# Two fused norm and projection stages: most of their opening loads are issued later, behind the first tile's expert rows

## The chip, the cores and the metric

One core of one Trainium2 chip runs the whole program as one launch. The time is that of the device in microseconds, median of several runs. The engines are TensorE (PE in the profile), VectorE (DVE), ScalarE (ACT), GpSimd (POOL) and SyncE (SP). SP and ACT issue ordinary DMAs, POOL issues the indirect ones (gathers). All of them move their bytes through the same 16 DMA engines.

## The reference, cut to what matters

Two transformer blocks of depth two and one, over 1024 tokens of width 1024 in float32. Each layer is a mixer (attention and the like), a norm, a mixture of experts and a norm. The change touches two places, each between the experts of one layer and the mixer of the next:

```python
y = hierarchical_moe(h, ...)                        # out[token] = g0 * rows[p0] + g1 * rows[p1]
x = layer_norm(ALPHA * x + (1 + g2) * y, ln_g, ln_b)
# next layer
h = x * (1 + sc1) + sh1
qkv = h @ w_qkv                                     # or h @ w_in in the third layer
```

Every token has two rows among the experts' outputs, at places that the router found at run time. `g2`, `sc1` and `sh1` are vectors of 1024 numbers that `front` computed and left in DRAM, `ln_g` and `ln_b` are inputs.

## The kernel before, in words

The program is a row of stages, each with its own buffers and semaphores and with a barrier of all engines at its end. The two stages of this change are `norm_qkv` (stage `n1`, lines 811 to 1081) and `norm_mix` (stage `n3`, lines 1084 to 1429). Each starts after an experts stage and works through 8 tiles of 128 tokens. For each tile `t`:

1. POOL gathers the tile's two expert rows per token, `z` and `y2` (L884, L1171), 0.52 MB each. From `t = 2` on it first waits until the norm's output of tile `t - 2` has been stored, since that lies in `y2` (semaphore `x_st`).
2. ACT scales `z` by the first gate (`weigh`, L937, L1261). DVE adds `y2` times the second (L1010, L1364), multiplies by `gate` (L1015, L1369), adds alpha times `x` (L1017, L1371), takes the statistics and normalises (`combine`).
3. DVE makes two results: `xt`, the shaped input of the projection (L1028, L1382), and `y2`, the norm's output (L1030, L1384). PE turns `xt` by transposes (`turn_h`), ACT copies it (`spread_h`), and PE projects it with the weights `wt` (`project`). ACT keeps the result, and DVE works on it: `rope` in `norm_qkv`, ending at L1071, `norm_latents` in `norm_mix`, ending at L1410. PE turns what they leave (`turn_qk`, `turn_lat`).

For tile 0, DVE also adds 1 to `gate` (L1013, L1367) and folds the five constants together (`shape_next`, L1035 to L1038, L1389 to L1392), before `xt` and `y2` can be made.

The order of the loads is written out by hand. SP issues in this order: `places`, `gates`, `x` of tiles 0 and 1, the constants `gate`, `g`, `b`, `bs`, `gs` (0.52 MB each, since one row is spread over 128 partitions), `ident`, the weights in 3 or 4 column groups (6.3 and 6.8 MB), the rotation tables and gains (in `norm_mix` behind the first group of weights), in `norm_mix` also `uq` and `ukv`. Then comes a loop over the tiles, which stores the norm's output (`x_out`, L869, L1151) and loads `x` of tile `t + 2`. An instruction of this queue that doesn't find room, or waits, holds all behind it.

ACT works in a fixed order, too: in each turn of its loop `weigh(t + 2)` comes first, and the copies of tile `t`'s products come behind it. So do DVE and PE: in `norm_qkv` DVE does `combine(t + 2)` and then `rope(t)`, in `norm_mix` it does `norm_latents(t)` and then `combine(t + 2)`. PE does in `norm_qkv` `project(t, 0)`, `project(t, 1)`, `turn_qk(t - 1)`, `turn_h(t + 1)`, `project(t, 2)`, and in `norm_mix` `project(t, 0)`, `turn_q(t - 1)`, `project(t, 1)`, `turn_lat(t)`, and so on.

Of the kernel before, what the change touches and what calls it, by code (L numbers as in the profile page):

```python
# [16 lines left out]
P = 128  # L17
# [793 lines left out]
def norm_qkv(nc, name, x, mod, part, ln_g, ln_b, alpha, x_out, experts, nxt, w, q_gain, k_gain, a, qT, kT, v, scale):  # L811
# [6 lines left out]
    row = lambda m, n: m[0, n * D:(n + 1) * D].partition_broadcast(P)  # L818
    out_rows = x_out.rearrange("(r g c) n -> g r c n", g=TILES, c=GRID_W // TILES)
    with Stage(nc, name) as st:  # L820
# [12 lines left out]
        id_in, e_in, c_in, t_in, tables, shaping = (st.sem(n) for n in ("id_in", "e_in", "c_in", "t_in", "tables", "shaping"))  # L833
        w_in = [st.sem(f"w_in{c}") for c in range(GROUPS)]
        x_in, y_in, x_st = ([st.sem(f"{n}{j}") for j in range(2)] for n in ("x_in", "y_in", "x_st"))
        ready, weighted, nv, rt, sd, h_ready, x_ready = (st.sem(n) for n in ("ready", "weighted", "nv", "rt", "sd", "h_ready", "x_ready"))
        turned, evac, mm_done, qkv_cp, squared = (st.sem(n) for n in ("turned", "evac", "mm_done", "qkv_cp", "squared"))
        rv, roots, rope_done = (st.sem(n) for n in ("rv", "roots", "rope_done"))
# [11 lines left out]
        with st.block() as block:  # L850

            @block.sync
            def _(sp):
                sp.dma_start(places[:, :, :], experts[1]).then_inc(e_in, 16)
                sp.dma_start(gates[:, :, :], experts[2]).then_inc(e_in, 16)
                for j in range(2):
                    sp.dma_start(xt[:, j], x[j * P:(j + 1) * P, :]).then_inc(x_in[j], 16)
                for dst, src in ((gate, row(mod, part)), (g, ln_g.partition_broadcast(P)), (b, ln_b.partition_broadcast(P)),
                                 (bs, row(nxt[0], nxt[1])), (gs, row(nxt[0], nxt[1] + 1))):
                    sp.dma_start(dst[:, :], src).then_inc(c_in, 16)  # L860
                sp.dma_start(ident[:, :], a["ident"]).then_inc(id_in, 16)
                for c in range(GROUPS):
                    sp.dma_start(wt[:, :, c * 512:(c + 1) * 512], w.rearrange("(c p) n -> p c n", p=P)[:, :, c * 512:(c + 1) * 512]).then_inc(w_in[c], 16)
                for dst, src in ((cos[:, 0], rows(a["cos_grid"])), (sin[:, 0], rows(a["sin_grid"])),
                                 (gain[:, 0], q_gain.partition_broadcast(P)), (gain[:, 1], k_gain.partition_broadcast(P))):
                    sp.dma_start(dst, src).then_inc(t_in, 16)
                for t in range(TILES):
                    sp.wait_ge(x_ready, t + 1)
                    sp.dma_start(out_rows[t], y2[:, t % 2]).then_inc(x_st[t % 2], 16)  # L869
                    if t + 2 < TILES:  # L870
                        sp.wait_ge(turned, fills["h", t, 1] + 1)
                        sp.dma_start(xt[:, t % 2], x[(t + 2) * P:(t + 3) * P, :]).then_inc(x_in[t % 2], 16)
                for j in range(2):
                    sp.wait_ge(x_st[j], 16 * TILES // 2)

            @block.gpsimd
            def _(pool):
                pool.wait_ge(e_in, 32)
                for t in range(TILES):
                    if t >= 2:  # L880
                        pool.wait_ge(x_ready, t - 1)
                        pool.wait_ge(x_st[t % 2], 16 * (t // 2))
                    for k, dst in enumerate((z, y2)):
                        pool.indirect_dma_start(out=dst[:, t % 2], out_offset=None, in_=experts[0],  # L884
                                                in_offset=bass.IndirectOffsetOnAxis(ap=places[:, k, t:t + 1], axis=0)).then_inc(y_in[t % 2], 16)

            @block.tensor
            def _(pe):
# [115 lines left out]
            def _(dve):  # L1004
                step, shaped, turning = steps(dve, nv, 0), steps(dve, sd, 0), steps(dve, rv, 0)

                def combine(t):
                    j = t % 2
                    dve.wait_ge(weighted, t + 1)
                    step(dve.scalar_tensor_tensor(z[:, j], y2[:, j], gates[:, 1, t:t + 1], z[:, j], ALU.mult, ALU.add))  # L1010
                    if t == 0:
                        dve.wait_ge(c_in, 16 * 5)
                        dve.tensor_scalar(gate[:, :], gate[:, :], 1.0, None, ALU.add).then_inc(ready, 1)  # L1013
                        dve.wait_ge(ready, 1)
                    step(dve.tensor_tensor(z[:, j], z[:, j], gate[:, :], ALU.mult))  # L1015
                    dve.wait_ge(x_in[j], 16 * (t // 2 + 1))
                    step(dve.scalar_tensor_tensor(z[:, j], xt[:, j], alpha, z[:, j], ALU.mult, ALU.add))  # L1017
                    step(dve.bn_stats(bn[:, j, 0], z[:, j, 0:HALF]))
                    step(dve.bn_stats(bn[:, j, 1], z[:, j, HALF:]))
                    step(dve.bn_aggr(mv[:, j], bn[:, j]))  # L1020
                    step(dve.tensor_scalar(inv[:, j:j + 1], mv[:, j, 1:2], LN_EPS, None, ALU.add))
                    step(dve.reciprocal(inv[:, j:j + 1], inv[:, j:j + 1]))
                    if t == 0:
                        shape_next()
                    dve.wait_ge(rt, t + 1)
                    shaped(dve.tensor_scalar(z[:, j], z[:, j], mv[:, j, 0:1], rstd[:, j:j + 1], ALU.subtract, ALU.mult))
                    shaped(dve.tensor_tensor(xt[:, j], z[:, j], gs[:, :], ALU.mult))
                    dve.tensor_tensor(xt[:, j], xt[:, j], bs[:, :], ALU.add).then_inc(h_ready, 1)  # L1028
                    shaped(dve.tensor_tensor(y2[:, j], z[:, j], g[:, :], ALU.mult))
                    dve.tensor_tensor(y2[:, j], y2[:, j], b[:, :], ALU.add).then_inc(x_ready, 1)  # L1030

                def shape_next():

                    shape = steps(dve, shaping, 0)
                    shape(dve.tensor_scalar(gs[:, :], gs[:, :], 1.0, None, ALU.add))  # L1035
                    shape(dve.tensor_tensor(out[:, 0:D], b[:, :], gs[:, :], ALU.mult))
                    shape(dve.tensor_tensor(bs[:, :], bs[:, :], out[:, 0:D], ALU.add))
                    shape(dve.tensor_tensor(gs[:, :], gs[:, :], g[:, :], ALU.mult))  # L1038
# [45 lines left out]
def norm_mix(nc, name, x, mod, part, ln_g, ln_b, alpha, x_out, experts, nxt, w, q_gain, kv_gain, w_uq, w_ukv, a, padded, qT, kT, v, scale):  # L1084
# [9 lines left out]
    with Stage(nc, name) as st:  # L1094
# [16 lines left out]
        id_in, e_in, c_in, t_in, u_in, shaping = (st.sem(n) for n in ("id_in", "e_in", "c_in", "t_in", "u_in", "shaping"))  # L1111
        w_in = [st.sem(f"w_in{c}") for c in range(GROUPS)]
        x_in, y_in, x_st, v_st = ([st.sem(f"{n}{j}") for j in range(2)] for n in ("x_in", "y_in", "x_st", "v_st"))
        ready, weighted, nv, rt, sd, h_ready, x_ready = (st.sem(n) for n in ("ready", "weighted", "nv", "rt", "sd", "h_ready", "x_ready"))
        turned, evac, mm_done, pr_cp, lat_cp, summed = (st.sem(n) for n in ("turned", "evac", "mm_done", "pr_cp", "lat_cp", "summed"))
        lv, lat_root, lat_ready, up_done, up_cp, qv, q_ready = (st.sem(n) for n in ("lv", "lat_root", "lat_ready", "up_done", "up_cp", "qv", "q_ready"))
# [9 lines left out]
        with st.block() as block:  # L1126

            @block.sync
            def _(sp):
                sp.dma_start(places[:, :, :], experts[1]).then_inc(e_in, 16)  # L1130
                sp.dma_start(gates[:, :, :], experts[2]).then_inc(e_in, 16)
                for j in range(2):
                    sp.dma_start(xt[:, j], x[j * P:(j + 1) * P, :]).then_inc(x_in[j], 16)
                for dst, src in ((gate, row(mod, part)), (g, ln_g.partition_broadcast(P)), (b, ln_b.partition_broadcast(P)),
                                 (bs, row(nxt[0], nxt[1])), (gs, row(nxt[0], nxt[1] + 1))):
                    sp.dma_start(dst[:, :], src).then_inc(c_in, 16)
                sp.dma_start(ident[:, :], a["ident"]).then_inc(id_in, 16)
                for c in range(GROUPS):
# [22 lines left out]
            @block.gpsimd  # L1161
            def _(pool):
                pool.memset(zero[:, :], 0.0).then_inc(zeroed, 1)
                pool.memset(latn[:, :], 0.0).then_inc(blank, 1)
                pool.wait_ge(e_in, 32)
                for t in range(TILES):
                    if t >= 2:
                        pool.wait_ge(x_ready, t - 1)
                        pool.wait_ge(x_st[t % 2], 16 * (t // 2))
                    for k, dst in enumerate((z, y2)):  # L1170
                        pool.indirect_dma_start(out=dst[:, t % 2], out_offset=None, in_=experts[0],  # L1171
                                                in_offset=bass.IndirectOffsetOnAxis(ap=places[:, k, t:t + 1], axis=0)).then_inc(y_in[t % 2], 16)

            @block.tensor
            def _(pe):
# [182 lines left out]
            def _(dve):  # L1358
                step, shaped, latent, turning = steps(dve, nv, 0), steps(dve, sd, 0), steps(dve, lv, 0), steps(dve, qv, 0)

                def combine(t):
                    j = t % 2
                    dve.wait_ge(weighted, t + 1)
                    step(dve.scalar_tensor_tensor(z[:, j], y2[:, j], gates[:, 1, t:t + 1], z[:, j], ALU.mult, ALU.add))  # L1364
                    if t == 0:
                        dve.wait_ge(c_in, 16 * 5)
                        dve.tensor_scalar(gate[:, :], gate[:, :], 1.0, None, ALU.add).then_inc(ready, 1)  # L1367
                        dve.wait_ge(ready, 1)
                    step(dve.tensor_tensor(z[:, j], z[:, j], gate[:, :], ALU.mult))  # L1369
# [16 lines left out]
                def shape_next():  # L1386

                    shape = steps(dve, shaping, 0)
                    shape(dve.tensor_scalar(gs[:, :], gs[:, :], 1.0, None, ALU.add))  # L1389
                    shape(dve.tensor_tensor(y2[:, 0], b[:, :], gs[:, :], ALU.mult))  # L1390
                    shape(dve.tensor_tensor(bs[:, :], bs[:, :], y2[:, 0], ALU.add))
# [1694 lines left out]
```

## Time and profile before

| | us |
|---|---|
| median of 3 runs | 4115.12 (4114.41 to 4116.6) |
| the profiled execution | 4115.45 |
| its span | 4113.5 |
| PE busy (matmul) | 3484.4, 85% of the span |
| DVE busy | 1571.3, 38% |
| ACT busy | 873.8, 21% |
| DMA, mean over the span | 205 GB/s |
| stage `n1`, first instruction | 1347.12 |
| stage `n3`, first instruction | 2779.69 |

The profiled execution is 0.33 us above the median of the runs, inside their spread. PE is the busiest engine over the whole, but in the first 32 us of both stages it has nothing to do, and what counts there is when loads land.

### The profile page before, as it was taken

The numbers are of one execution on the slowest core, as the hardware profiler recorded it, in microseconds if no ns is written. First come the engines' busy times: TensorE is split into PE (matmuls) and PEld (weight loads), VectorE is DVE, ScalarE is ACT, GpSimd is POOL, SyncE is SP. The second block draws the span as 40 slices with busy tenths as digits, with TensorE's granted clock in tenths as the row PEclk, the third lists the DMA queues.
The fourth block names the chain that finished last, engine by engine and source line by source line (L and its number), as shares of the span: only waits on it lengthen the run. The fifth ranks groups of instructions, "written<-read, shape, count | busy, mean of one in ns | idle before, by whom it ended". The sixth has DMA issues, their size and how long they took to land. (4 is left out here: it accounts for less than half of the span.)

```text
span 4113.5 us, 48036 instructions
## 1 busy us (share of the span) xinstructions
PE 3484.4 (85%) x18756; PEld 1936.0 (47%) x18756; DVE 1571.3 (38%) x2595; ACT 873.8 (21%) x1896; POOL 235.5 (6%) x250
## 2 busy tenths in 40 slices
PE   7998988499999598999874999985999657847994
PEld 3444644144444244777442444433556456425662
DVE  4641755200000674666452000004426673551114
ACT  0001721011111123555110101002335322001112
POOL 1002000200000100000002000001000000011001
PEclk9999998699999799999986999997999878968997
DMA  9963031599996610000316999956210310419994
GB/s 379 357 220 122 7 130 66 209 427 426 426 422 256 201 57 1 1 1 2 140 56 239 427 426 427 421 227 213 88 46 23 112 46 22 159 36 366 420 390 195
DMA packets 176908, 842.26 MB, mean 205 GB/s; under 512 B 53455, under 2 KB 60367, under 8 KB 130610
## 3 DMA queue, kind: packets, MB, share of 16 engines
q1 hardware_dynamic: 142434, 737.83, 44.8%
q0 software_dynamic: 20576, 54.16, 3.6%
q10 hardware_dynamic: 13680, 47.24, 2.9%
q8 instruction: 152, 2.49, 0.2%
q14 instruction: 66, 0.54, 0.0%
HBM read 758.39 MB, written 97.20 MB: 208 GB/s over the span
## 5 line engine op out<-in xcount | busy, mean ns | idle before, releaser
L395 PE MATMUL front_acc<-front_hT,front_wt 128*128 128x512 f32 x512 | 224.8, 601 | 5.5 <-DMA front_wt<-in_na_w_qkv 5.5
L1215 PE MATMUL n_acc<-n_wt,n_hT 128*128 128x512 f32 (+2 forms) x512 | 191.3, 531 | 0.7 <-ACT n_hT L1255 0.7
L201 DVE TENSOR_REDUCE gqa_top<-gqa_scores 128x1 f32<-128x1024 f32 x128 | 150.8, 1220 | 101.5 <-PE gqa_scores L149 101.5
L232 ACT ACTIVATE gqa_probs<-gqa_scores,gqa_top 128x1024 f32<-128x1024 f32 x128 | 142.5, 1113 | 168.2 <-DVE gqa_top L201 168.2
L2137 PE MATMUL m1x_gp<-m1x_w,m1x_xT 128*128 128x512 f32 (+1 forms) x512 | 171.9, 600 | 1.5 <-issue 0.7
L2137 PE MATMUL m0x_gp<-m0x_w,m0x_xT 128*128 128x512 f32 (+1 forms) x512 | 171.4, 599 | 1.5 <-issue 0.7
L2162 PE MATMUL m1x_yp<-m1x_w,m1x_hidT 128*128 128x512 f32 (+1 forms) x512 | 169.3, 594 | 2.1 <-ACT m1x_hidT L2223 2.1
L2162 PE MATMUL m0x_yp<-m0x_w,m0x_hidT 128*128 128x512 f32 (+1 forms) x512 | 169.3, 594 | 2.1 <-ACT m0x_hidT L2223 2.1
L2137 PE MATMUL m0x_up<-m0x_w,m0x_xT 128*128 128x512 f32 (+1 forms) x512 | 168.8, 593 | 0.0
L2137 PE MATMUL m1x_up<-m1x_w,m1x_xT 128*128 128x512 f32 (+1 forms) x512 | 168.8, 593 | 0.0
L913 PE MATMUL n_acc<-n_wt,n_hT 128*128 128x512 f32 x384 | 168.2, 598 | 0.7 <-ACT n_hT L931 0.7
L395 PEld LDWEIGHTS front_acc<-front_hT,front_wt 128*128 128x128 f32 x512 | 97.9, 193 | 131.8 <-issue 131.1
L468 DVE SCALAR_TENSOR_TENSOR front_total<-v,front_cact,front_total 128x2048 f32<-128x2048 f32 x56 | 131.6, 2350 | 64.3 <-DMA v<-in_ada_w 44.8
L139 PE MATMUL gqa_turn<-gqa_ident,gqa_probs 128*128 128x128 f32 x1024 | 139.9, 280 | 0.8 <-DVE gqa_probsT L190 0.7
L2277 DVE TENSOR_TENSOR m1x_hid<-m1x_sg,m1x_up 128x512 f32<-128x512 f32 x24 | 16.5, 687 | 320.7 <-PE m1x_up L2137 320.7
L2277 DVE TENSOR_TENSOR m0x_hid<-m0x_sg,m0x_up 128x512 f32<-128x512 f32 x24 | 16.5, 688 | 320.2 <-PE m0x_up L2137 320.2
L139 PEld LDWEIGHTS gqa_turn<-gqa_ident,gqa_probs 128*128 128x128 f32 x1024 | 109.4, 140 | 60.0 <-issue 59.1
L1215 PEld LDWEIGHTS n_acc<-n_wt,n_hT 128*128 128x128 f32 x512 | 98.2, 194 | 82.9 <-issue 77.8
L149 PE MATMUL gqa_scores<-k1T,q1T 64*128 64x512 f32 x512 | 131.0, 627 | 5.9 <-DMA gqa_ident<-in_ident 3.4
L168 PE MATMUL gqa_out<-gqa_probsT,v 128*64 128x128 f32 x2048 | 125.9, 276 | 0.8 <-ACT gqa_probsT L228 0.8
L1707 PE MATMUL n_acc<-n_wt,o1T 128*128 128x512 f32 x256 | 112.9, 601 | 14.8 <-DMA n_wt<-in_gqa_w_o 14.8
L1707 PE MATMUL n_acc<-n_wt,mixT 128*128 128x512 f32 x256 | 112.7, 600 | 15.0 <-DMA n_wt<-in_w_out 15.0
(617 smaller groups left out, 5469.6 us busy)
## 6 DMA issues: line engine op xcount, KB each, us to landing
m0x_w<-in_moe_w_gate SPq DMA_DIRECT2D x32, 2048.0 KB, 33.3
m0x_w<-in_moe_w_up SPq DMA_DIRECT2D x32, 2048.0 KB, 33.2
m0x_w<-in_moe_w_down SPq DMA_DIRECT2D x32, 2048.0 KB, 33.4
m1x_w<-in_moe_w_gate SPq DMA_DIRECT2D x32, 2048.0 KB, 32.7
m1x_w<-in_moe_w_up SPq DMA_DIRECT2D x32, 2048.0 KB, 32.7
m1x_w<-in_moe_w_down SPq DMA_DIRECT2D x32, 2048.0 KB, 33.2
v<-in_ada_w SPq DMA_DIRECT2D x40, 1024.0 KB, 12.4
m2x_w<-in_moe_w_gate SPq DMA_DIRECT2D x32, 1024.0 KB, 32.2
```

Of the source, the lines that this page charges most:

```text
L139: last = pe.transpose(turn[f % TURN][:, i * P:(i + 1) * P], src, ident[:, :])
L149: last = pe.matmul(scores[h][:, c * 512:(c + 1) * 512], qT[half, j, t * P:(t + 1) * P], kT[half, 2 * j // SHARE, c * 512:(c + 1) * 512], s ...
L168: pe.matmul(out[h * HEAD:(h + 1) * HEAD, 0:P], v[:, k, kv * HEAD:(kv + 1) * HEAD], probsT[:, n % 2, h, k], start=k == 0, stop=k == TILES - 1)
L201: dve.tensor_reduce(top[:, n % 2, h:h + 1], scores[h][:, :], AX.X, ALU.max, negate=True).then_inc(max_ready, 1)
L232: act.activation(probs[:, n % 2, h], scores[h][:, :], ACT.Exp, bias=top[:, n % 2, h:h + 1], accum_out=total[:, n % 2, h:h + 1]).then_inc(p ...
L395: last = pe.matmul(acc[n % 4][:, :], wt[:, c % 2, k, i * P:(i + 1) * P], hT[:, k, half * 512:(half + 1) * 512], start=k == 0, stop=k == KC ...
L468: dve.scalar_tensor_tensor(total[:, q % 2], mw[:, s % RING], by, total[:, q % 2], ALU.mult, ALU.add).then_inc(weighed, 1)
L913: last = pe.matmul(acc[t % 2][:, c], hT[:, t % 2, k], wt[:, k, c * 512:(c + 1) * 512], start=k == 0, stop=k == KC - 1)
L1215: last = pe.matmul(acc[c][:, 0:n1 - n0], hT[:, t % 2, k], wt[:, k, n0:n1], start=k == 0, stop=k == KC - 1)
L1707: last = pe.matmul(acc[t % 2][:, c * HALF:(c + 1) * HALF], srcT[:, place(k), t * P:(t + 1) * P], wt[:, k, c * HALF:(c + 1) * HALF], start= ...
L2137: last = pe.matmul(acc[r, 0:F], xT[:, j, k, r], w[:, q % RING, k * F:(k + 1) * F], start=k == 0, stop=k == KC - 1)
L2162: last = pe.matmul(yp[e][r, :], hidT[:, k, r], w[:, q % RING, k * D + e * 512:k * D + (e + 1) * 512], start=k == 0, stop=k == FC - 1)
```

## The change

Both stages get two semaphores, `asked` and `gate_in`. POOL raises `asked` once it has issued the two gathers of tile 0. SP issues `places`, `gates` and `x` of tile 0, waits for `asked`, issues `gate` alone (counted by `gate_in`), waits until both gathers of tile 0 have landed (`y_in[0]` at 32), and only then issues `x` of tile 1, the other four constants (now `gs` first), `ident`, the weights and all the rest in the old order. DVE waits for `gate` alone where it waited for all five constants, and for the other four at the head of `shape_next`. Nothing is computed otherwise.

The part of `norm_qkv`; that of `norm_mix` is the same with its own lines (L1133 to L1138, L1171, L1366, L1388):

```diff
+        asked, gate_in = st.sem("asked"), st.sem("gate_in")
...
                 sp.dma_start(places[:, :, :], experts[1]).then_inc(e_in, 16)
                 sp.dma_start(gates[:, :, :], experts[2]).then_inc(e_in, 16)
-                for j in range(2):
-                    sp.dma_start(xt[:, j], x[j * P:(j + 1) * P, :]).then_inc(x_in[j], 16)
-                for dst, src in ((gate, row(mod, part)), (g, ln_g.partition_broadcast(P)), (b, ln_b.partition_broadcast(P)),
-                                 (bs, row(nxt[0], nxt[1])), (gs, row(nxt[0], nxt[1] + 1))):
+                sp.dma_start(xt[:, 0], x[0:P, :]).then_inc(x_in[0], 16)
+                sp.wait_ge(asked, 1)
+                sp.dma_start(gate[:, :], row(mod, part)).then_inc(gate_in, 16)
+                sp.wait_ge(y_in[0], 32)
+                sp.dma_start(xt[:, 1], x[P:2 * P, :]).then_inc(x_in[1], 16)
+                for dst, src in ((gs, row(nxt[0], nxt[1] + 1)), (g, ln_g.partition_broadcast(P)), (b, ln_b.partition_broadcast(P)),
+                                 (bs, row(nxt[0], nxt[1]))):
                     sp.dma_start(dst[:, :], src).then_inc(c_in, 16)
                 sp.dma_start(ident[:, :], a["ident"]).then_inc(id_in, 16)
                 for c in range(GROUPS):
...
                     for k, dst in enumerate((z, y2)):
                         pool.indirect_dma_start(...).then_inc(y_in[t % 2], 16)
+                    if t == 0:
+                        pool.sem_inc(asked, 1)
...
                     if t == 0:
-                        dve.wait_ge(c_in, 16 * 5)
+                        dve.wait_ge(gate_in, 16)
                         dve.tensor_scalar(gate[:, :], gate[:, :], 1.0, None, ALU.add).then_inc(ready, 1)
...
                 def shape_next():
                     shape = steps(dve, shaping, 0)
+                    dve.wait_ge(c_in, 16 * 4)
```

## Rows read from the trace of the kernel before

**Rows 1.** Waits of PE in both stages: who for whom, total us, times, longest
```profile
PE n_turn L894 <- DVE n_xt L1028: 46.0, 1, 46.0
...
PE n_turn L1181 <- DVE n_xt L1382: 45.5, 1, 45.5
```
**Rows 2.** Timeline, opening of `n1`: start, us, engine, line, [idle before <-releaser]
```profile
1347.98 0.90 SPq L857 DMA_DIRECT2D n_xt<-sc_x  x2
...
1349.36 0.96 POOL L884 DMA_INDIRECT n_z<-sc_expert_rows,n_places  x1 [98.26 <-DMA n_gates<-sc_gates]
...
1350.64 0.96 POOL L884 DMA_INDIRECT n_y<-sc_expert_rows,n_places  x1 [0.31 <-issue]
...
1351.90 15.62 SPq L863 DMA_DIRECT2D n_wt<-in_gqa_w_qkv  x3
...
1360.83 1.15 ACT L937 ACTIVATE n_z<-n_z,n_gates 128x1024 f32<-128x1024 f32 x1 [27.16 <-DMA n_y<-sc_expert_rows,n_places]
...
1365.63 0.69 DVE L1013 TENSOR_SCALAR n_gate<-n_gate 128x1024 f32<-128x1024 f32 x1 [2.34 <-DMA n_gs<-sc_mod]
...
1370.97 0.69 DVE L1035 TENSOR_SCALAR n_gs<-n_gs 128x1024 f32<-128x1024 f32 x1
...
1378.95 1.94 PE L894 MATMUL n_turn<-n_ident,n_xt 128*128 128x128 f32 x8 [45.98 <-DVE n_xt L1028]
```
**Rows 3.** Windows: us, busy of five engines, PEclk, DMA share, GB/s
```profile
1349.00:1351.00 2.00, 0.00 (x0) 0.00 (x0) 0.00 (x0) 0.00 (x0) 1.33 (x2) 0.50 0.83 285
...
1353.00:1355.00 2.00, 0.00 (x0) 0.00 (x0) 0.00 (x0) 0.00 (x0) 0.95 (x1) 0.50 1.03 330
...
1361.00:1363.00 2.00, 0.00 (x0) 0.00 (x0) 0.99 (x1) 0.98 (x1) 0.00 (x0) 0.50 1.02 418
...
1367.00:1381.00 14.00, 1.94 (x8) 1.56 (x8) 13.52 (x16) 2.09 (x4) 0.00 (x0) 0.50 1.05 386
...
1390.00:1392.00 2.00, 2.00 (x6) 0.90 (x5) 1.97 (x3) 0.00 (x0) 0.24 (x1) 1.00 0.76 254
...
2804.00:2807.00 3.00, 0.00 (x0) 0.00 (x0) 2.90 (x4) 0.00 (x0) 0.00 (x0) 0.50 0.31 62
...
2835.00:2838.00 3.00, 0.00 (x0) 0.00 (x0) 0.98 (x8) 2.36 (x8) 0.00 (x0) 0.50 0.42 168
```
**Rows 4.** Timeline of `n1` behind its opening, same columns
```profile
1382.58 0.63 SPq L869 DMA_DIRECT2D sc_x<-n_y  x1
...
1387.73 1.25 POOL L884 DMA_INDIRECT n_z<-sc_expert_rows,n_places  x1 [33.63 <-DMA sc_x<-n_y]
...
1394.43 1.15 ACT L937 ACTIVATE n_z<-n_z,n_gates 128x1024 f32<-128x1024 f32 x1 [7.19 <-DMA n_y<-sc_expert_rows,n_places]
...
1396.28 1.28 DVE L1010 SCALAR_TENSOR_TENSOR n_z<-n_y,n_gates,n_z 128x1024 f32<-128x1024 f32 x1
...
1416.21 0.75 DVE L1071 TENSOR_TENSOR n_out<-n_qk,n_rn 128x256 f32<-128x256 f32 x2
...
1418.72 1.04 PE L894 MATMUL n_turn<-n_ident,n_out 128*128 128x128 f32 x8
```
**Rows 5.** Groups of instructions by line, `n1`, PE: busy, mean ns | idle before
```profile
L913 PE MATMUL n_acc<-n_wt,n_hT 128*128 128x512 f32 x384 | 168.2, 598 | 0.7 <-ACT n_hT L931 0.7
```
**Rows 6.** Timeline of `n3`, same columns
```profile
2782.14 0.97 POOL L1171 DMA_INDIRECT n_z<-sc_expert_rows,n_places  x1 [1.28 <-DMA n_gates<-sc_gates]
...
2785.01 10.28 SPq L1144 DMA_DIRECT2D n_cos<-in_cos_line  x1
...
2798.24 0.69 DVE L1367 TENSOR_SCALAR n_gate<-n_gate 128x1024 f32<-128x1024 f32 x1 [2.23 <-DMA n_gs<-sc_mod]
...
2816.95 0.35 SPq L1151 DMA_DIRECT2D sc_x<-n_y  x1
...
2827.80 0.94 POOL L1171 DMA_INDIRECT n_z<-sc_expert_rows,n_places  x1 [40.93 <-DMA sc_x<-n_y]
...
2838.77 0.90 PE L1194 MATMUL n_turn<-n_ident,n_latn 128*128 128x128 f32 x3 [9.55 <-DVE n_latn L1410]
```

More of the change, by code:

```diff
@@ L1113, in norm_mix @@
         x_in, y_in, x_st, v_st = ([st.sem(f"{n}{j}") for j in range(2)] for n in ("x_in", "y_in", "x_st", "v_st"))
+        asked, gate_in = st.sem("asked"), st.sem("gate_in")
         ready, weighted, nv, rt, sd, h_ready, x_ready = (st.sem(n) for n in ("ready", "weighted", "nv", "rt", "sd", "h_ready", "x_ready"))
@@ L1131, in _ @@
                 sp.dma_start(gates[:, :, :], experts[2]).then_inc(e_in, 16)
[L1132 to L1135, printed above, removed]
+                sp.dma_start(xt[:, 0], x[0:P, :]).then_inc(x_in[0], 16)
+                sp.wait_ge(asked, 1)
+                sp.dma_start(gate[:, :], row(mod, part)).then_inc(gate_in, 16)
+                sp.wait_ge(y_in[0], 32)
+                sp.dma_start(xt[:, 1], x[P:2 * P, :]).then_inc(x_in[1], 16)
+                for dst, src in ((gs, row(nxt[0], nxt[1] + 1)), (g, ln_g.partition_broadcast(P)), (b, ln_b.partition_broadcast(P)),
+                                 (bs, row(nxt[0], nxt[1]))):
                     sp.dma_start(dst[:, :], src).then_inc(c_in, 16)
@@ L1172, in _ @@
                                                 in_offset=bass.IndirectOffsetOnAxis(ap=places[:, k, t:t + 1], axis=0)).then_inc(y_in[t % 2], 16)
+                    if t == 0:
+                        pool.sem_inc(asked, 1)
             @block.tensor
@@ L1365, in combine @@
                     if t == 0:
-                        dve.wait_ge(c_in, 16 * 5)
+                        dve.wait_ge(gate_in, 16)
                         dve.tensor_scalar(gate[:, :], gate[:, :], 1.0, None, ALU.add).then_inc(ready, 1)
@@ L1388, in shape_next @@
                     shape = steps(dve, shaping, 0)
+                    dve.wait_ge(c_in, 16 * 4)
                     shape(dve.tensor_scalar(gs[:, :], gs[:, :], 1.0, None, ALU.add))
```

## The prediction

> **What bounds the kernel now.** I read first who waited for whom on PE. In each of the two stages PE waits once for a long time, 46.0 and 45.5 us, for the first shaped tile [rows 1]. Most of that is the end of the stage before, but the last 30 us are this stage's own opening, and there the change works. Next I read the timeline of that opening [rows 2]. The first gathers are issued at 1349.36 and 1350.64. ACT can begin with their rows at 1360.83, 11.5 us after the first issue. DVE adds its part and stands idle for 2.34 us, because the one wait covers all five constants, and the last of them, `gs`, lets it go at 1365.63. The statistics follow, `shape_next` starts at 1370.97, and PE gets its first transposes at 1378.95. Then I read how fast bytes flow [rows 3]: 330 to 418 GB/s while gathers and loads mix, 386 GB/s through 14 us of weights, but only 254 GB/s at 1390, where the gathers of tile 2 are nearly alone. So in the opening the DMA engines are full. In such a stretch a delayed load doesn't make bytes disappear: whatever time the engines stand idle is added to all that queues behind. This is the main point of what follows.
>
> Last I followed what hangs on the end of that queue. In `n1` [rows 4] SP comes to the first `x_out` at 1382.58, behind the weights and tables. Its landing releases the gathers of tile 2 at 1387.73, ACT's `weigh(2)` starts when they have landed at 1394.43, and DVE takes the tile up at 1396.28. `rope(0)`, which stands behind that tile on DVE, ends at 1416.21 + 0.75 = 1416.96, and PE wants its result at 1418.72. Otherwise PE's projections hardly wait: 0.7 us before all 384 records of L913 [rows 5]. In `n3` the same chain is late already: `x_out` issued at 2816.95, gathers at 2827.80, and at 2838.77 PE begins `turn_lat(0)` after 9.55 us of idleness [rows 6]. That wait runs through DVE's `norm_latents(0)` to ACT's copy of tile 0, which stands behind `weigh(2)` on ACT, and that waits for the gathers of tile 2.
>
> **The change, part by part.**
>
> *The first gathers land sooner.* Alone, a pair of gathers takes 1394.43 - 1387.73 = 6.7 us from the first issue to ACT's start [rows 4]. In the changed `n1` they have only `x` of tile 0 ahead and `gate` beside them. From 1349.36 that gives 1356.1 at the least. If `gate`'s 0.52 MB went wholly ahead of them, at some 0.36 MB/us, it would add 1.4 us, and nothing if it ran in the gaps that gathers leave; I take 0.9, so 1357.0. The upper end is the time of before, 1360.8.
>
> *The DVE chain for tile 0.* From ACT's start to the start of `shape_next` it takes 1370.97 - 1360.83 - 2.34 = 7.8 us without the wait. From 1357.1 it is at `shape_next` at 1364.9.
>
> *The constants land later.* Ahead of DVE's old wait lie 11 transfers of 0.524 MB: two of `x`, five constants, four gathers, together 5.77 MB. They are still the same 11 in the changed kernel. When tile 0's rows land at 1357.0, four have passed (`x`, `gate`, two gathers: 2.10 MB). Now SP must see the semaphore, issue, and the first bytes must come. In the opening the loads of `x` were issued at 1347.98, and the next window moves 285 GB/s for 2 us [rows 2, 3], 0.57 MB, which at 0.40 MB/us is 1.4 us of flow; so bytes began at about 1349.6, 1.6 us after the issue. I take 1.5. In that gap only tile 1's gathers flow, at 0.25 MB/us [rows 3]: 0.38 MB. From 1358.5 the remaining 5.77 - 2.10 - 0.38 = 3.29 MB go at 0.40 MB/us, between the 418 and the 386 GB/s of [rows 3], in 8.2 us. Last bytes at 1366.7, DVE released 0.5 us later at 1367.2, against 1365.63 before. So **the whole queue slips by 1.6 us**. I call this the slip. Its low end is about 0.1 us (rows at 1356.1, restart after 1 us, 418 GB/s throughout), its high end 4.5 us (rows as late as before, 1360.8, then 1.5 us, then the rest at 0.40, of which between 2.6 and 3.3 MB is left: 3.7 to 5.3). Below nothing it can hardly be, since the engines had no idle time to give back.
>
> *Start of PE.* `shape_next` waits for the later of 1364.9 and 1367.2. It starts at 1367.2, 3.8 us sooner than at 1370.97. `root(0)` on ACT stands behind `weigh(1)`; tile 1's rows should land by 1362, so it doesn't bind. The first transposes come at 1375.2. The first group of weights is the next thing that could be late: it follows `gs` and `ident` in the queue, needs 2.1 MB at 386 GB/s, 5.4 us, and lands at about 1373; PE needs it at 1378. It is covered, by 5 us. The second and third follow 5.4 us apart each, while PE spends about 7 us or more on a group.
>
> *What becomes of the 3.8 us in `n1`.* SP reaches the first `x_out` when weights and tables have made room in its queue, so 1.6 us later. With the slip, `weigh(2)` starts at 1396.0 and ends at 1397.2. DVE began this tile at 1396.28, having been itself the later one by 1396.28 - 1394.43 - 1.19 = 0.66 us. It now begins at 1397.2, 0.9 later. So `rope(0)` ends at 1417.9, and PE, which by its own work would be there at 1414.9, waits until 1418.0 instead of starting at 1418.72. Gain 0.8 us. In general it is 0.66 + 1.76 (1418.72 - 1416.96) - slip = 2.4 - slip. Behind that point the order is PE's again, and the 0.8 stays. **n1: 0.8 us gained.**
>
> *What becomes of it in `n3`.* The same sum from 2782.14: rows at 2789.7, restart at 2791.2, constants at 2799.9 against 2798.24, a slip of 1.7 us. `uq`, `ukv` and `x_out` stand behind all the weights, so the gathers of tile 2 come 1.7 us later than 2827.80, and PE's `turn_lat(0)` 1.7 us later than 2838.77. PE reaches this wait 3.7 us sooner and waits it all away. The longer idleness costs nothing in clock, because the granted clock has fallen to 0.50 (1.2 GHz) by 2835 already [rows 3] and PE starts from there before and after. **n3: 1.7 us lost.**
>
> *Small things.* One semaphore increment on POOL ahead of tile 1's gathers, two waits on SP, one on DVE, two more semaphores to clear in each stage: 0 to 0.2 us together by the 0.03 us between neighbouring DVE steps; they lie beside waits for DMAs. I take nothing. What queues behind SP's new waits is everything that SP loads and stores; behind DVE's wait in `shape_next` stand the rest of tile 0 and tile 1, and PE and ACT's `spread_h(0)` wait for them.
>
> Sum: -0.8 + 1.7 = +0.9 us, which is 2 x slip - 2.4 rounded. Against the profiled execution 4115.45 becomes 4116.4; against the median of the runs, 0.33 lower, 4116.0.
>
> *A rule of the notes.* The pair of gathers of tile 2 took 6.7 us for 1.05 MB [rows 4]. The Trainium skill, "DMA: Bandwidth & Descriptors", section "Anatomy of one DMA", gives a fixed part of about 2.0 us and the bytes at 436 GB/s, 4.4 us for these bytes; the trace disagrees, and the row is used. By the page's figure the rows would be there 2.3 us sooner, the slip would be nearer to 1.0 us (an estimate from that page), and the sum would be -0.4. The same section says that a wait for a semaphore is kept by the engine that issues, so that a held load pays its fixed part after the wait; that speaks against this change, and the 1.6 us from the issue of `x` to its bytes agrees.
>
> **The rivals.** *The gain carries.* If tile 2's gathers didn't hang on the queue's end, both stages would keep the earlier start: 3.8 + 3.7 = 7.5 us, 4107.6; with the DVE chain as the only limit (1364.9) up to 12 us, 4103. For it speaks that PE hardly waits after the start [rows 5]; against it the chain to 1418.72 in `n1`, with 1.76 us of slack, and the 9.55 us in `n3` [rows 4, 6]. 0.14.
>
> *The gathers hardly get faster.* If the 11.5 us are mostly POOL's and the rows' own, the slip is 4.5 us and the sum 2 x 4.5 - 2.4 = +6.6: 4121.7. For it speaks that at the start of gathers the engines moved only 330 GB/s though full of work; against it the 6.7 us alone. 0.12.
>
> *SP becomes the bound (the other side).* SP comes to the first weights not at 1351.90 but at 1357.1 + 7 issues of 0.49 = 1360.5, 8.6 us later, in both stages. If descriptors were made only as SP gets on, everything behind would be 8.6 us late: `n1` loses 8.6 - 2.4 = 6.2, `n3` 8.6, 14.8 together: 4129.9. It decides from the point at which this delay exceeds the time for which SP was held anyway: 10.28 - 0.45 = 9.8 us at `cos` in `n3`, and 15.62 - 3 x 0.5 = 14.1 us in the three weight issues of `n1` [rows 2, 6]. 8.6 is below both, though in `n3` by 1.2 us only. For it speaks the hole at 2804 to 2807, 62 GB/s with DMAs to come [rows 3]: there the queue did run dry once. 0.10.
>
> **How the numbers follow.** Forecast as summed, 4116.0, with its own 4112 to 4120: 0.64. The measurement tells 0.2% from no change, 8.2 us, so it calls faster what is below 4106.9 and slower what is above 4123.3. The forecast and the slow gathers lie within it almost wholly (0.75), of the carried gain half (0.07) lies below, and SP as the bound is slower but for a weak form (0.09), with 0.01 for a slower form of the slow gathers. Faster 0.07, same 0.83, slower 0.10. The range takes in the forecast, the slow gathers at 4121.7 and the nearer half of the carried gain: 4107 to 4122.
>
> **What would show it.** In the changed profile: ACT's first `weigh` near 1357 and 2790; DVE idle not before `gate` but before `shape_next`, for some 2 us; PE's first transposes 3 to 4 us sooner; the first `x_out` of `n1` 1 to 2 us later; PE idle before `turn_qk(0)` for 3 us where it had none; PE's wait before `turn_lat(0)` in `n3` grown from 9.6 to about 15 us, and its start near 2840.5 (less what `n1` gave). I am wrong if `x_out` comes no later or sooner, since then the DMA engines had more to give than I read, or if a group of weights stops PE.

## The result, and the profile after

The changed kernel takes 4124.3 us (median of 15 runs, 4120.45 to 4129.27), the kernel before in the same rounds 4115.37 (15 runs, 4111.88 to 4118.25). The ratio is 1.0022 with an interval of 1.0014 to 1.003: 8.9 us or 0.22% slower, with an interval wholly above 1. The forecast was 4116.0 with a range of 4107 to 4122, so the time lies above the range. The profiled execution took 4124.07 us, its span 4121.9 against 4113.5 before. The head of the page of the changed kernel shows the same work as before: 18756 matmuls and as many weight loads, 2595 instructions on DVE, 1896 on ACT.

```profile
span 4121.9 us, 48040 instructions
...
PE 3490.7 (85%) x18756; PEld 1936.2 (47%) x18756; DVE 1571.1 (38%) x2595; ACT 873.8 (21%) x1896; POOL 235.2 (6%) x250
```

I cut both traces at the first `places` load of each stage. Of the 8.4 us between the spans, `n1` holds 3.4 (241.67 us long against 238.27), the unchanged stages between it and the first `m1` stage 1.3 (562.97 against 561.66), `n3` 3.0 (310.28 against 307.28), all the rest 0.7. Times below that are called *offsets* count from that first load, which in `n1` lies at 1347.12 before and 1347.37 after, in `n3` at 2779.69 and 2784.89.

The opening of `n1` after, from the timeline (start, duration, engine, line; idle time before it and what ended it in brackets). It answers to [rows 2] and [rows 4]:

```profile
1349.58 0.32 SPq L859 DMA_DIRECT2D n_gate<-sc_mod  x1
1349.77 0.96 POOL L888 DMA_INDIRECT n_z<-sc_expert_rows,n_places  x1 [98.33 <-DMA n_gates<-sc_gates]
...
1357.95 0.32 SPq L861 DMA_DIRECT2D n_xt<-sc_x  x1
1358.03 1.15 ACT L943 ACTIVATE n_z<-n_z,n_gates 128x1024 f32<-128x1024 f32 x1 [24.01 <-DMA n_y<-sc_expert_rows,n_places]
...
1370.05 0.69 DVE L1042 TENSOR_SCALAR n_gs<-n_gs 128x1024 f32<-128x1024 f32 x1 [4.22 <-DMA n_bs<-sc_mod]
...
1378.03 1.94 PE L900 MATMUL n_turn<-n_ident,n_xt 128*128 128x128 f32 x8 [44.71 <-DVE n_xt L1034]
...
1386.74 0.63 SPq L873 DMA_DIRECT2D sc_x<-n_y  x1
...
1391.82 1.14 POOL L888 DMA_INDIRECT n_z<-sc_expert_rows,n_places  x1 [37.33 <-DMA sc_x<-n_y]
1392.17 0.56 SPq L873 DMA_DIRECT2D sc_x<-n_y  x1
...
1399.45 1.15 ACT L943 ACTIVATE n_z<-n_z,n_gates 128x1024 f32<-128x1024 f32 x1 [13.14 <-DMA n_y<-sc_expert_rows,n_places]
...
1400.71 1.28 DVE L1016 SCALAR_TENSOR_TENSOR n_z<-n_y,n_gates,n_z 128x1024 f32<-128x1024 f32 x1 [5.35 <-ACT n_z L943]
...
1420.62 0.75 DVE L1078 TENSOR_TENSOR n_out<-n_qk,n_rn 128x256 f32<-128x256 f32 x2
...
1421.42 2.92 PE L900 MATMUL n_turn<-n_ident,n_out 128*128 128x128 f32 x12 [3.82 <-DVE n_out L1078]
```

Read it against the rows of before. Tile 0's rows come to ACT at 1358.03 instead of 1360.83, so the first gathers do land sooner. The last constant lets DVE go at 1370.05 instead of 1365.63, so that DVE stands idle for 4.22 us. PE's first transposes still begin 0.9 us sooner. Then the order turns round: the first `x_out` is issued at 1386.74 instead of 1382.58, the gathers of tile 2 at 1391.82 instead of 1387.73, and they take 7.63 us to ACT's start instead of 6.70. PE has no work left from 1417.60 and waits 3.82 us, where before it had no such wait.

The same chain in `n3`, after, to be read with [rows 6]:

```profile
2794.81 1.15 ACT L1274 ACTIVATE n_z<-n_z,n_gates 128x1024 f32<-128x1024 f32 x1 [22.92 <-DMA n_y<-sc_expert_rows,n_places]
...
2806.17 0.69 DVE L1403 TENSOR_SCALAR n_gs<-n_gs 128x1024 f32<-128x1024 f32 x1 [3.56 <-DMA n_bs<-sc_mod]
...
2825.27 0.35 SPq L1162 DMA_DIRECT2D sc_x<-n_y  x1
...
2835.64 0.94 POOL L1182 DMA_INDIRECT n_z<-sc_expert_rows,n_places  x1 [43.74 <-DMA sc_x<-n_y]
...
2846.55 0.90 PE L1207 MATMUL n_turn<-n_ident,n_latn 128*128 128x128 f32 x3 [15.13 <-DVE n_latn L1424]
```

By offsets: rows at 9.92 instead of 13.85, constants at 21.28 instead of 18.55, `x_out` at 40.38 instead of 37.26, gathers of tile 2 at 50.75 instead of 48.11, PE's `turn_lat(0)` at 61.66 instead of 59.08, after 15.13 us of idleness instead of 9.55.

Windows of the changed kernel (bounds, us, busy of PE, weight load, DVE, ACT, POOL, granted clock, DMA share, GB/s):

```profile
1351.00:1355.00 4.00, 0.00 (x0) 0.00 (x0) 0.00 (x0) 0.00 (x0) 2.85 (x3) 0.50 0.69 213
...
1359.00:1363.00 4.00, 0.00 (x0) 0.00 (x0) 3.69 (x4) 2.60 (x3) 0.00 (x0) 0.50 0.97 359
1363.00:1366.00 3.00, 0.00 (x0) 0.00 (x0) 2.65 (x6) 0.14 (x1) 0.00 (x0) 0.50 1.01 239
1366.00:1370.00 4.00, 0.00 (x0) 0.00 (x0) 0.00 (x0) 0.06 (x1) 0.00 (x0) 0.50 1.02 374
...
1416.00:1418.00 2.00, 1.60 (x4) 0.38 (x2) 1.93 (x5) 0.72 (x2) 0.84 (x1) 1.00 0.00 0
...
1420.00:1422.00 2.00, 0.58 (x3) 0.58 (x4) 2.00 (x4) 0.00 (x0) 0.26 (x1) 0.80 0.80 248
1422.00:1424.00 2.00, 2.00 (x11) 1.71 (x9) 1.93 (x3) 1.17 (x2) 0.00 (x0) 0.50 0.59 211
...
2800.00:2803.00 3.00, 0.00 (x0) 0.00 (x0) 2.44 (x6) 0.20 (x1) 0.00 (x0) 0.50 1.01 261
```

and of the kernel before, in the first of these stretches:

```profile
1351.00:1355.00 4.00, 0.00 (x0) 0.00 (x0) 0.00 (x0) 0.00 (x0) 2.49 (x3) 0.50 1.04 365
```

Two things are to be seen. While SP holds its loads back, the DMA engines are busy for 0.69 of the time and move 213 GB/s; in the same stretch of the kernel before they were full and moved 365. And from 1363 to 1366, when the share is 1.01 again, they move only 239. The lines from 1416 to 1424 belong to the clock, told below.

### The profile page after: what moved, and what is told of

It is laid out like the page before. It is cut to its first block and busy times, and to the rows that moved or that the text cites. A ratio compares the mean times of both kernels' runs of the same rounds, so it can differ in the third digit from the quotient of the medians.

```text
span 4121.9 us, 48040 instructions
## 1 busy us (share of the span) xinstructions
PE 3490.7 (85%) x18756; PEld 1936.2 (47%) x18756; DVE 1571.1 (38%) x2595; ACT 873.8 (21%) x1896; POOL 235.2 (6%) x250
## 5 line engine op out<-in xcount | busy, mean ns | idle before, releaser
L2291 DVE TENSOR_TENSOR m0x_hid<-m0x_sg,m0x_up 128x512 f32<-128x512 f32 x24 | 16.5, 687 | 321.6 <-PE m0x_up L2151 321.6
L2291 DVE TENSOR_TENSOR m1x_hid<-m1x_sg,m1x_up 128x512 f32<-128x512 f32 x24 | 16.5, 687 | 321.1 <-PE m1x_up L2151 321.1
```

## The experiments

### Each stage alone

`only_n1` has the change in `norm_qkv` alone, `only_n3` in `norm_mix` alone; the other function is that of the kernel before.

> The change in norm_qkv (n1) alone; norm_mix is that of before. Theory A (the queue of SP slips, and the tile that waits for the first x_out carries the slip on): in the profile of the changed kernel n1 took 3.35 us more from its first instruction to the next stage, so this kernel is 3 to 5 us slower than before, about 4119, with PE idle for some 4 us before turn_qk(0), and n3 of its old length, 307.3 us. Theory B (the loss comes from something common, such as the longer program or more semaphores, and not from the two openings): the time stays within 1 us of the changed kernel's or of before.

> The change in norm_mix (n3) alone. Theory A: n3 takes 2.6 to 3.0 us more, PE's wait before turn_lat(0) grows from 9.6 to about 15 us, and the program is 3 to 4 us slower than before. The sum of this and of n1 alone is the loss of the whole change, about 8 us. Theory B: no change against before, or the whole 8 us.

`only_n1` took 4122.57 us and `only_n3` 4119.95 against 4116.9 for the kernel before: ratios 1.0011 (1.0002 to 1.002) and 1.0008 (0.9999 to 1.0017). That is 5.7 and 3.05 us, 8.7 together, the whole loss. The interval of `only_n3` reaches just below 1, so its time alone doesn't tell it from the kernel before; its trace does. `only_n1` lost more than the 3 to 5 us expected, and 2.0 us of it lie in the unchanged stages behind `n1`. Lengths in the traces agree: `n3` is 2.8 us longer in `only_n3` (310.12) and 0.2 in `only_n1` (307.52), `n1` 4.5 us longer in `only_n1` (242.76) and 0.9 in `only_n3` (239.20); so one profiled execution differs from another by up to 1 us in such a stage. The waits of PE (who for whom, total us, times, longest), first `only_n1`:

```profile
PE n_turn L900 <- DVE n_out L1078: 13.8, 2, 10.7
...
PE n_turn L1201 <- DVE n_latn L1417: 9.2, 1, 9.2
```

and `only_n3`:

```profile
PE n_turn L1200 <- DVE n_latn L1417: 15.1, 1, 15.1
```

In `only_n1` the wait of `n3` is the 9 us of before, and in `n1` a second wait of 13.8 - 10.7 = 3.1 us has come to the old one of 10.7. So each of the two losses is made in its own stage, with one addition: with the new `n1` the unchanged GQA stage behind it is longer as well (below).

### The order and the split wait, without the hold

`no_hold` keeps the new order of loads, the separate semaphore of `gate` and DVE's later wait, and takes the hold away:

```
-                sp.wait_ge(asked, 1)
                 sp.dma_start(gate[:, :], row(mod, part)).then_inc(gate_in, 16)
-                sp.wait_ge(y_in[0], 32)
...
-                    if t == 0:
-                        pool.sem_inc(asked, 1)
```

> The changed kernel without SP's two waits: the new order (x of tile 0, gate, x of tile 1, gs, g, b, bs) and DVE's split wait stay, but nothing is held. Theory A (the hold makes the slip): the first x_out of both stages comes within 0.5 us of before, counted from the stage's start, tile 0's rows land as late as before (11.5 us after the first gather), and the time is that of before within 2 us. Rival C (the order, or the split of the wait, costs): still 4 us or more slower than before.

4119.52 us, ratio 1.0007 (0.9998 to 1.0016), and a profiled span of 4116.4. Its timeline, `shape_next` and the first `x_out` of both stages:

```profile
1370.93 0.69 DVE L1038 TENSOR_SCALAR n_gs<-n_gs 128x1024 f32<-128x1024 f32 x1
...
1384.91 0.63 SPq L871 DMA_DIRECT2D sc_x<-n_y  x1
...
2820.57 0.35 SPq L1156 DMA_DIRECT2D sc_x<-n_y  x1
```

Its `n1` begins at 1349.29, so `shape_next` starts at offset 21.64 instead of 23.85, with no idle time of DVE before it, and `x_out` is issued at 35.62 against 35.46 before. In `n3` they are 21.53 and 37.77, against 23.88 and 37.26. So the 2.2 to 2.35 us by which the tile's first part moves up come from the order and the split wait alone, and the slip of `x_out` (3.9 and 3.1 us) comes from the hold: without it 0.2 and 0.5 remain. In `n1` `shape_next` starts 1.0 us sooner here than with the hold (22.68), in `n3` 0.25 us later (21.28). The hold buys tile 0's rows and then makes their user wait for the constants. The time was expected within 2 us of the kernel before; it is 2.6 us above it, with an interval that takes in 1. So the order alone costs little or nothing, and it gains nothing either, though PE starts 2.2 and 2.3 us sooner: PE then waits 1.72 us before `turn_qk(0)`, and 12.55 instead of 9.55 us before `turn_lat(0)`. The trace has `n1` 0.5 us shorter than before, `n3` 0.1, and the stages behind `n1` 1.5 us longer.

### Where the slip comes from

The forecast slip was 1.6 us; the constants came 4.2 and 2.7 us later. Three kernels look at the 3 us at 239 and 261 GB/s, in which only loads of one row to 128 partitions are under way. `ln_rows` reads `ln_g` and `ln_b` from arrays that hold the row 128 times:

```
-                for dst, src in (..., (g, ln_g.partition_broadcast(P)), (b, ln_b.partition_broadcast(P)), ...
+                for dst, src in (..., (g, ln_g), (b, ln_b), ...
...
+        inputs[name + "_rows"] = np.repeat(inputs[name][:, 1:2], P, axis=1)
```

> The changed kernel, but g and b of both stages are read from inputs that hold 128 copies of their row, one for each partition, instead of one row that 128 partitions read. The holds stay. Theory D (of the 4.2 us by which the constants land later in n1, some 2 us come from g and b: with no gathers beside them the DMA engines were full but moved only 0.20 to 0.27 MB/us for 3 us, because all read one row): those 3 us disappear, the constants are there 1.5 to 2 us sooner in n1 and 1 to 1.5 us in n3, and the kernel is 2.5 to 4 us faster than the changed one, about 4121. Rival E (the low rate has another cause, such as the start of the queue after the hold): the rate stays at 0.20 to 0.27 MB/us and the time is that of the changed kernel.

`all_rows` takes `gs` and `bs` from such an array too, that of `ln_b`. It leaves out the real scale and shift, so what it computes is not the layer, and only its openings are read:

```
+                for dst, src in ((gs, ln_b), (g, ln_g), (b, ln_b), (bs, ln_b)):
```

> As the run with 128 copies of g and b, but gs and bs are read from those copies too (their values are wrong, so what is computed from them is left out of the comparison; only the openings are read). Theory D: with no load of one row behind the hold, 4 KB packets take 160 to 180 ns throughout, and the constants are there 20 to 20.7 us after the stage's start in n1, against 22.7 in the changed kernel and 22.0 with g and b alone; what is left of the slip, 1.5 to 2.2 us against 18.5, is the idle time of the hold, and agrees with the 1.6 us of the prediction. Rival E: a stretch with packets of 250 to 300 ns and 0.2 MB/us stays, and the constants land at 22.

`half_hold` leaves the one-row loads of `g` and `b` beside the gathers and holds only what follows:

```
+                for dst, src in ((g, ln_g.partition_broadcast(P)), (b, ln_b.partition_broadcast(P))):
+                    sp.dma_start(dst[:, :], src).then_inc(c_in, 16)
                 sp.wait_ge(y_in[0], 32)
```

> The changed kernel, but g and b are issued ahead of SP's wait for tile 0's rows, beside gate and the gathers; x of tile 1, gs, bs and the rest stay behind it. Theory A with D (idle DMA time, and loads of one row that are slow by themselves but run for nothing beside gathers, make the slip): tile 0's rows land 1 to 2 us later than in the changed kernel, 11.5 to 12.5 us after the stage's start in n1, the slip of x_out falls from 3.9 to 1 to 2 us in n1 and from 3.1 to about 1 us in n3, and the kernel is 3 to 6 us faster than the changed one, 4118 to 4121. Against it (the slip is fixed by the wait itself, whatever is held): slip and time as in the changed kernel.

Measured, as offsets in `n1` / `n3`, with the ratio to the kernel before:

| kernel | tile 0's rows | `shape_next` | first `x_out` | time, ratio |
|---|---|---|---|---|
| before | 13.71 / 13.85 | 23.85 / 23.88 | 35.46 / 37.26 | 4115.37 |
| changed | 10.66 / 9.92 | 22.68 / 21.28 | 39.37 / 40.38 | 4124.3, 1.0022 |
| `ln_rows` | 10.79 / 10.69 | 21.97 / 21.16 | 38.70 / 40.08 | 4123.39, 1.0016 (1.0007 to 1.0025) |
| `all_rows` | 11.09 / 10.03 | 21.38 / 19.81 | 38.10 / 39.44 | 4121.15, one run |
| `half_hold` | 13.18 / 13.48 | 22.06 / 22.47 | 38.79 / 41.58 | 4123.23, 1.0016 (1.0007 to 1.0025) |

Windows of `all_rows` at the place of the slow stretch, same columns as above:

```profile
1364.00:1367.00 3.00, 0.00 (x0) 0.00 (x0) 2.90 (x4) 0.89 (x1) 0.00 (x0) 0.50 0.92 318
1367.00:1370.00 3.00, 0.00 (x0) 0.00 (x0) 0.69 (x4) 0.20 (x1) 0.00 (x0) 0.50 1.01 376
...
2800.00:2803.00 3.00, 0.00 (x0) 0.00 (x0) 2.86 (x5) 0.51 (x1) 0.00 (x0) 0.50 0.98 384
```

With separate rows the slow stretch is gone: 318 GB/s at a share of 0.92 in `n1`, where there were 239 at 1.01, and 384 GB/s where there were 261 in `n3`. The constants come 1.3 and 1.5 us sooner than in the changed kernel and the first `x_out` 1.3 and 0.9. So about 1.2 us of the slip is the one-row loads left alone by the hold. The constants of `n1` were expected at 20 to 20.7 and came at 21.38, so more is left of the slip than was expected. `ln_rows` gave only 0.7 and 0.1, and `gs` and `bs` were still one-row loads there. So `ln_rows` by itself would have spoken against the one-row loads; `all_rows` decided for them.

The slip that is left in `all_rows`, 2.6 and 2.2 us at `x_out`, goes with the hold's idle time: 0.69 of the engines busy at 213 GB/s instead of 365 for 4 us makes 0.61 MB less, 1.5 us at 0.40 MB/us. With the slow stretch's 0.48 MB that is 1.1 MB, and 1.12 MB is what the changed kernel's engines have moved less by offset 22 us of `n1` (6.40 against 7.52), some 2.8 us. What `x_out` is later beyond that, 1.1 us of the 3.9 in `n1`, I haven't traced to a cause.

`half_hold` missed. Its `g` and `b` went beside the gathers, so tile 0's rows came nearly as late as before, while `x_out` came 0.6 us sooner than in the changed kernel in `n1` and 1.2 us later in `n3`. Half the hold costs what the whole one costs. Its trace of `n1` still has both stretches, 280 GB/s from 1351 to 1355 and 254 from 1364 to 1367; that these are the gap of the wait and the one-row loads behind it is likely, but no run shows it apart.

### The store that the queue's end holds back

If the loss goes from the queue's end through `x_out` to the gathers of tile 2, it must vanish when `x_out` doesn't stand in SP's queue. `pool_store_before` and `pool_store_after` are the two kernels with `x_out` issued by POOL:

```
-                    sp.wait_ge(x_ready, t + 1)
-                    sp.dma_start(out_rows[t], y2[:, t % 2]).then_inc(x_st[t % 2], 16)
...
+                def store(t):
+                    pool.wait_ge(x_ready, t + 1)
+                    pool.dma_start(out_rows[t], y2[:, t % 2]).then_inc(x_st[t % 2], 16)
...
-                        pool.wait_ge(x_ready, t - 1)
+                        store(t - 2)
```

> The kernel before, with one part moved in both stages: POOL issues the stores of the norm's output itself, right before the gathers that wait for them, where SP issued them behind all weights and tables. Theory A (the loss of the change goes through this one store): in n3 the gathers of tile 2 start 5 to 9 us sooner than 48.1 us after the stage's start, PE's wait of 9.6 us before turn_lat(0) shrinks to 0 to 4 us, and the kernel is 4 to 9 us faster than before, 4108 to 4113. In n1, where the store left SP's queue 1.4 us after it could, 0 to 2 us. Rival B (the gathers wait for something else): no change.

> The changed kernel with the same move. Theory A: the slip of SP's queue no longer reaches the gathers of tile 2, so the loss of 8 us goes, and what is left is the earlier start of PE, 1.2 us in n1 and 2.6 us in n3: between 4 us faster than the kernel before with the same move and equal to it. Rival F (the weights or the tables, which land 4 and 3 us later, are the next to stop PE or DVE, or tile 2's x, which SP still loads behind them, does): 2 us or more slower than the kernel before with the same move, with a new wait for one of these loads.

4114.86 us without the change (ratio to the kernel before 0.9994, 0.9985 to 1.0003) and 4111.51 with it (0.9988, 0.9979 to 0.9997). `pool_store_before` was expected 4 to 9 us faster than the kernel before and is 2.1, with an interval that takes in 1: in `n3` the gathers of tile 2 are issued 6.0 us sooner, but PE's wait before `turn_lat(0)` only shrinks from 9.55 to 6.59 us. The timeline of `pool_store_after`, with the stores on POOL:

```profile
1381.42 0.60 POOL L882 DMA_DIRECT2D sc_x<-n_y  x1 [25.39 <-DVE n_y L1040]
...
1388.24 1.95 POOL L890 DMA_INDIRECT n_z<-sc_expert_rows,n_places  x1 [6.21 <-DMA sc_x<-n_y]
...
1418.60 1.09 PE L904 MATMUL n_turn<-n_ident,n_out 128*128 128x128 f32 x8
...
2816.22 0.60 POOL L1178 DMA_DIRECT2D sc_x<-n_y  x1 [26.78 <-DVE n_y L1405]
...
2824.14 0.97 POOL L1188 DMA_INDIRECT n_z<-sc_expert_rows,n_places  x1 [7.32 <-DMA sc_x<-n_y]
```

Its waits of PE:

```profile
PE n_turn L904 <- DVE n_out L1082: 10.7, 1, 10.7
```

`x_out` now follows DVE, at offset 32.47 instead of 39.37, and the second wait behind the 10.7 is gone: PE has no gap at 1418.60. The stage `n1` is 236.33 us long, against 238.59 in `pool_store_before`, and the change costs nothing any more, where it cost 8.9 us. That shows the path of the loss. It doesn't cure all of it: `n3` is 304.14 us long against 303.63, and the stages from GQA to the next `m1` 563.59 against 561.57. Whether the early start is then worth something is less sure: in the repeat below `n1` was 238.11 us long.

Two more runs ask whether the hold has a part in that. `pool_store_no_hold` is `no_hold` with POOL's stores, `pool_store_after_2` is `pool_store_after` again, measured beside it.

> The kernel without holds (new order of the loads, split wait of DVE, nothing held), with the stores of the norm's output issued by POOL. It asks whether the hold itself is worth anything once nothing waits for the end of SP's queue. If the earlier first tile comes from the split wait and the order (without holds the constants were folded 21.6 and 21.5 us after the stages' starts, with them 22.7 and 21.3), this kernel is within 2 us of the changed kernel with POOL's stores, about 4111 to 4113. If the hold gives the gain, it is 2 us or more slower than that one.

> The changed kernel with POOL's stores once more, beside the one without holds on the same chip: between 4 and 7 us faster than the kernel before.

4112.53 (ratio 0.999, 0.9981 to 0.9999) and 4114.32 (0.9993, 0.9984 to 1.0002). The repeat was expected 4 to 7 us under the kernel before and is 2.3 under it; it came out 2.8 us above its first measurement, so differences of 2 to 3 us between these kernels mean nothing. What stands: with POOL's stores the new order is as fast without the hold as with it, 2 to 5 us under the kernel before of the same rounds, where the changed kernel was 8.9 us above it; 2.1 us of that came with the moved store alone. `pool_store_no_hold` and the first measurement of `pool_store_after` have intervals wholly below 1; the repeat's reaches just above it.

In `n3` of `pool_store_after` the moved store brought less than it promised: the gathers of tile 2 are issued at offset 41.84 instead of 50.75 but need 9.9 us, beside the weights that are still flowing, where they needed 6.6, so ACT has the rows at 51.77 instead of 57.36 and PE begins at 56.06 instead of 61.66.

## Why the prediction came out as it did

**The gathers land sooner: right, a little less than said.** Forecast for ACT's start 1357.1; it was 1358.03, of which 0.25 is the later stage. In `n3` 2794.81 - 2787.17, with the first gather at 2787.17, is 7.6 us, just as forecast; in `n1` it was 1358.03 - 1349.77 = 8.3. The wait for `asked` did not put `gate` behind the gathers: it is issued 0.19 us before the first of them. The 4.4 us by the Trainium skill ("DMA: Bandwidth & Descriptors", section "Anatomy of one DMA") are further off than the row was. What I made of that figure was wrong as well: by my own sum, rows that land 2.3 us sooner bring the constants 2.3 us sooner too, which takes the slip from 1.6 us to nothing and not to 1.0. And the 1.6 us from the issue of `x` to its bytes can't be called an agreement with the page, since the same section puts most of its fixed part behind the last byte; no run here takes the two apart.

**The DVE chain: right.** From ACT's start DVE was ready for `shape_next` at 1370.05 - 4.22 = 1365.83, that is 7.8 us.

**The slip: the step that failed.** I wrote that "the whole queue slips by 1.6 us", with DVE released at 1367.2. It was 1370.05. Of these 2.85 us, 0.9 is the later landing of the rows. The rest is the rate: I let the remaining bytes flow at 0.40 MB/us; they flowed at 0.359 for 4 us, 0.239 for 3 us and 0.374 for 4 us, which is 0.16 + 0.48 + 0.10 = 0.74 MB short, 1.9 us at 0.40. I had taken 0.40 from stretches in which one-row loads were mixed with gathers, or weights flowed; the change makes the one-row loads run by themselves, and no window that I had of before showed that case. The range of the slip (0.1 to 4.5) did hold the 4.2, but I tied its upper end to late rows, one cause out of several, and gave it only the small chance of that rival. "Below nothing it can hardly be" was right, and for the reason given: the engines had nothing to give back.

**What the slip does in `n1`: the formula right, with two terms missing.** Forecast was a gain of 2.4 less the slip. `weigh(2)` came 4.77 us later by offsets: 3.84 for the gathers' issue, and 0.93 because the pair took 7.63 us instead of 6.70. In the changed kernel the `x_out` of tile 1 is issued at 1392.17, between the two gathers; in the 3.7 us from that pair's first issue the loads and stores of SP's queue moved 0.45 MB and the gathers nothing. So it is likely this store that slows them, but no run took it away alone. `pool_store_after` shows that it needn't be this store: there the pair took 8.37 us, with 0.69 MB of SP's loads in its first 4.3 us, and 6.87 us in `pool_store_no_hold`, with 0.27 MB in the first 3.2. 4.77 - 2.4 = 2.4, and PE began `turn_qk(0)` 2.45 us later. So instead of 0.8 gained, 2.45 were lost.

The second missing term is the clock. I treated the wait before `turn_qk(0)` as costing its own length. PE ran at a granted clock of 1.00 (2.4 GHz) until 1417.60 and stood for 3.82 us. The windows above show 0.80 and then 0.50 (1.2 GHz): in the trace the clock falls at 1421.2, just before PE takes up work at 1421.42, and is back at 1424.6. By the end of the next projections the loss was 3.4 us instead of 2.45: 0.9 for the clock. The sentence "the longer idleness costs nothing in clock" was true for `n3`, where the clock was at 0.50 already, and I had not asked the same question of the new wait in `n1`.

**`n3`: right in kind, 1.7 forecast, 2.6 at PE and 3.0 in the stage's length.** "PE reaches this wait 3.7 us sooner and waits it all away" is what happened: 2.6 us sooner, 15.13 us of idleness where I had said about 15. The slip at the gathers was 2.64 us, and PE was late by 2.58.

**A term outside the two stages.** The GQA stage behind `n1`, with no line changed, took 402.11 us against 400.65. Its first 50 us after the change, from the changed kernel's windows:

```profile
1589.00:1639.00 50.00, 45.50 (x351) 29.32 (x352) 26.99 (x39) 24.65 (x46) 0.00 (x0) 0.87 0.01 2
```

and at the same place of the kernel before:

```profile
1585.40:1635.40 50.00, 44.90 (x376) 29.76 (x378) 28.43 (x41) 25.87 (x49) 0.00 (x0) 0.92 0.01 2
```

PE is as busy, does 351 matmuls instead of 376, and its granted clock is 0.87 instead of 0.92. It stays at 1.00 from 16.5 us after the stage's first load to the stage's end, where it did so from 11.5 us. Over all the traces, the stages from GQA to the next `m1` took 562.75 to 563.97 us in the nine traces whose `n1` has any part of the new order, and 561.57 to 561.90 in the three with the old one (before, `only_n3`, `pool_store_before`); the clock comes to its lasting 1.00 after 13.5 to 16.6 us in the nine, after 11.5 to 12.0 in the three. Why the clock comes back later is open; the 1.3 us are in the measured time and were in no term of mine.

**The rivals.** *SP becomes the bound* had the right sign and a time 5.6 us too high, but it isn't what happened: SP's first `x_out` came 3.9 and 3.1 us later, not 8.6. *The gathers hardly get faster* gave 4121.7, nearer to the measured time than the forecast, by a slip of 4.5 us for which the cause named is wrong, since the rows did come sooner. *The gain carries* is refuted for this kernel by the traces of `only_n1` and `only_n3`, whose stages are longer though PE starts sooner; with the store moved, the two measurements of the new order lie 2.3 and 5.4 us under the kernel before, against 2.1 for the moved store alone, so at most a part of it comes through.

The sum of what was measured: 3.4 in `n1` (2.45 of chain, 0.9 of clock), 1.3 in the stages behind it, 3.0 in `n3`, 0.7 elsewhere, 8.4 in all, where 0.9 was forecast. Of the 7.5 us between them, 3.2 are the mis-sized slip (3.84 and 2.64 us at the gathers of tile 2 instead of 1.6 and 1.7), 0.9 the slower pair of gathers in `n1`, 0.9 the clock, 0.4 the rest of `n3` behind PE's start, and 2.0 lie outside both stages.

## What to carry to other kernels

Where the DMA engines are full, holding loads back to let one through doesn't reorder bytes for nothing: price the idle time of the hold, and price the held bytes by the rate they have when they run with nothing else, and add both to whatever stands last in that queue. Look for what hangs on the end of the queue before asking what starts sooner; here a single store behind all the loads of its stage decided, and with that store moved the same order and hold cost nothing that could be measured. A new wait of PE costs its length, and it can cost the clock on top: ask what the granted clock is at that place.

## What the runs showed of the hardware

- Loads of one row to 128 partitions, alone behind the hold in the changed kernel, moved 239 and 261 GB/s with the engines' share at 1.01. In the first of these stretches 200 packets passed in 3 us of 16 engines, 0.24 us each; with separate rows, in `all_rows`, 260 at a share of 0.92, 0.17 us each, and the rate in `n3` was 384 GB/s. In the kernel before, one-row loads ran beside gathers at 365 GB/s (1351 to 1355), so being one-row is not enough; what else makes them slow is open.
- A semaphore increment that POOL issues behind its indirect DMAs can be seen before they are: SP's `gate`, which waits for it, was issued at 1349.58, the first gather at 1349.77, and in `n3` at 2786.98 against 2787.17. It says nothing of whether the rows were asked for.
- In `n1` of the changed kernel the granted clock went from 1.00 to 0.50 near the end of 3.82 us without work and stayed there for 3.4 us, nearly all of them with PE working again. In `only_n1`, behind a wait of 3.03 us, it fell only when PE had been working for 1.6 us. Behind the waits of 1.72 us in `no_hold` and 2.42 us in `half_hold` it stayed at 1.00.
- SP's queue evened out a late start: in the changed kernel SP reached the weights of `n1` 9.5 us later (1361.43 instead of 1351.90) and came to `x_out` 4.2 us later (1386.74 instead of 1382.58). It stood for 10.26 us in issuing the three groups of weights, where before it had stood for 15.62.
